# Experts of a decoder layer: a ring of ten weight units, gathers without padding rows, results added into the output, down matrices issued by ScalarE

## The reference

```
h  = x + concat(rmsnorm(pooling mixer), rmsnorm(sparse attention), rmsnorm(memory attention)) @ w_out
hn = rmsnorm(h, g_ffn)
grp = argmax of softmax(hn @ w_router1 + b1)          # one of 4 groups
top 2 of the 8 experts of that group, weights = softmax(top 2) * p(grp)
y  = h + sum over the 2 chosen experts e of  weight * (silu(hn @ w_gate[e]) * (hn @ w_up[e])) @ w_down[e]
```

## Time and profile before

| | us |
|---|---|
| median of 3 runs (1293.37 to 1298.17) | 1296.27 |
| span of the profiled execution, first to last instruction | 1288.5 |
| `mix` begins | 580.8 |
| first gather of `experts` | 720.0 |
| last down product begins | 1253.1 |
| TensorE busy | 1060.3 |
| VectorE busy | 458.5 |
| moved by DMA | 294.33 MB |

### The profile page before, as it was taken

One profiled execution on the slowest core, in us unless ns is written; L12 is line 12 of the kernel. 1 busy time (PEld: TensorE's weight loads), 2 busy tenths in 40 slices (PEclk: granted clock), 3 DMA queues, 4 the chain that ended last, 5 costly groups with the idle time before them and its releaser, 6 DMA issues. The chain is left out here.

```text
span 1288.5 us, 16001 instructions
## 1 busy us (share of the span) xinstructions
PE 1060.3 (82%) x6275; PEld 694.2 (54%) x6275; DVE 458.5 (36%) x950; ACT 175.3 (14%) x415; POOL 71.2 (6%) x104
## 2 busy tenths in 40 slices
PE   5899979999996899988996498788887788877880
PEld 2455657777784677776455354444444444444440
DVE  3233313422424678653434322222222222222223
ACT  1021211111100344330001000000000000000000
POOL 0000030100100000000000100000000000000003
PEclk9999889999976799686996698999999999999995
DMA  9970083553100600004115279999999999999995
GB/s 396 266 231 25 13 199 99 154 141 98 50 1 2 253 1 1 1 1 196 69 63 231 81 284 401 403 400 408 409 404 407 405 407 410 406 413 415 407 382 207
DMA packets 58438, 294.33 MB, mean 228 GB/s; under 512 B 6992, under 2 KB 23183, under 8 KB 40783
## 3 DMA queue, kind: packets, MB, share of 16 engines
q1 hardware_dynamic: 35191, 255.76, 51.8%
q0 software_dynamic: 5280, 21.15, 5.2%
q10 hardware_dynamic: 17920, 16.78, 4.2%
HBM read 272.55 MB, written 25.42 MB: 231 GB/s over the span
## 5 line engine op out<-in xcount | busy, mean ns | idle before, releaser
L1751 PE MATMUL ps<-w_b,xTe 128*64 128x256 f32 x1024 | 132.0, 416 | 37.8 <-DMA w_b<-in_w_up 34.1
L1751 PE MATMUL ps<-w_a,xTe 128*64 128x256 f32 x1024 | 123.2, 397 | 27.0 <-DMA w_a<-in_w_up 24.9
L1813 DVE COPY xTe<-ps 128x512 f32<-128x512 f32 x32 | 22.1, 692 | 345.9 <-PE ps L1741 345.9
L829 PE MATMUL ps<-XT,w_a 128*128 128x126 f32 (+1 forms) x576 | 132.9, 409 | 5.7 <-DVE ht L564 5.7
L829 PEld LDWEIGHTS ps<-XT,w_a 128*128 128x128 f32 x576 | 120.4, 227 | 15.4 <-issue 6.3
L1751 PEld LDWEIGHTS ps<-w_b,xTe 128*64 128x64 f32 x1024 | 81.4, 150 | 83.9 <-DMA w_b<-in_w_up 40.9
L1751 PEld LDWEIGHTS ps<-w_a,xTe 128*64 128x64 f32 x1024 | 74.3, 142 | 71.3 <-DMA w_a<-in_w_up 30.8
L430 PE MATMUL ps<-w_b,xT 128*128 128x454 f32 (+1 forms) x240 | 81.1, 549 | 0.7 <-ACT z L402 0.7
L1856 ACT ACTIVATE gc<-gc 128x256 f32<-128x256 f32 x32 | 13.3, 416 | 450.2 <-DVE gc L1819 450.2
L1726 POOL DMA_INDIRECT xg<-hn_dram,table x32 | 28.8, 899 | 592.6 <-PE ps L1741 453.9
L1378 PE MATMUL ps<-w_b,mT 128*128 128x512 f32 x128 | 58.1, 614 | 1.9 <-ACT mT L1446 1.3
(11 more groups left out here) (362 smaller groups left out, 1308.5 us busy)
## 6 DMA issues: line engine op xcount, KB each, us to landing
w_a<-in_w_gate SPq DMA_DIRECT2D x16, 2048.0 KB, 17.2
w_a<-in_w_up SPq DMA_DIRECT2D x16, 2048.0 KB, 23.3
w_a<-in_w_down SPq DMA_DIRECT2D x16, 2048.0 KB, 12.5
w_b<-in_w_gate SPq DMA_DIRECT2D x16, 2048.0 KB, 16.6
w_b<-in_w_up SPq DMA_DIRECT2D x16, 2048.0 KB, 22.4
w_b<-in_w_down SPq DMA_DIRECT2D x16, 2048.0 KB, 13.2
w_a<-in_cache_kv SPq DMA_DIRECT2D x64, 256.0 KB, 5.1
ys_dram<-yb ACTq DMA_DIRECT2D x64, 128.0 KB, 7.8
```

The source lines that it names most:

```text
L829: ins = nc.tensor.matmul(hidv[:, 2 * q:2 * q + 2, 0:n], w1[:, q, l, :], XT[:, q, :, l:l + 8 * (n - 1) + 1:8], start=(l == 0), stop=(l == 15))
L1751: ins = nc.tensor.matmul(ps[h * CAP:h * CAP + CAP, bank, 0:FH], xT[:, slot, k, :], w[slot][:, k, h * FH:h * FH + FH], start=(k == 0), stop ...
L1813: nc.vector.tensor_copy(xT[:, slot, :, :].rearrange("p k s -> p (k s)"), ps[:, 4, 0:KD * CAP]).then_inc(xT_ready, 1)
```

## The change

What it does, part by part:

- **Ring.** Gate, up and down matrices of all experts become units u = 3n, 3n+1, 3n+2 in one ring of ten buffers: six in `w_a` and `w_b`, two in the space of `z`, two new ones (`more`) that exist only in the `experts` stage. For `z` to be free, GpSimd first copies the part of it that `mix` reads into `zu`, and TensorE and SyncE wait for that. Eight units are loaded in `mix` instead of six.
- **Who issues them.** SyncE issues gate and up units, ScalarE the down units from n = 3 on, behind its exponential of expert n-3.
- **Padding rows.** An unused slot now holds the number 2048 (the first slot of an expert 519), and gathers skip numbers above 519.
- **Adding scatter.** ScalarE multiplies the result by the slot's weight (`slot_w`) as it copies it. GpSimd then adds the 128 half rows of an expert (2 KB each, unused ones skipped) straight into `y` by an indirect transfer with `compute_op=ADD`. Each waits for the one before it to land. `mix` stores `h` to `y` for that.
- **Table.** The product that makes `table` also makes `slot_w`, and both for 128 partitions: 96 columns and 40 passes where there were 48 and 20. The first two gathers are issued at the end of `mix`.
- **Gone.** `combine`, the `h_dram` and `ys_dram` buffers, and the clearing write. `overflow` moves into the `experts` stage. The loops over experts are written out.

The places stand in this order: `mix` (SyncE, GpSimd, TensorE), the two new transfers, then `experts` (SyncE, GpSimd, ScalarE).

```diff
-            wg, wu, wd = self.expert_slot(self.w_a)
-            self.load_gate_up(sp, 0, 0, (wg, wu))
-            self.load_down(sp, 0, 0, wd)
+            for u in range(3):
+                self.load_unit(sp, u)
+            sp.wait_ge(u_kept, 2)
+            for u in range(6, 8):
+                self.load_unit(sp, u)
...
+            nc.gpsimd.tensor_copy(zu[:, 0:TILES, :], z[:, 0:TILES, U0:U0 + 256]).then_inc(u_kept, 1)
+            nc.gpsimd.tensor_copy(zu[0:NB, TILES, :], z[0:NB, TILES, U0:U0 + 256]).then_inc(u_kept, 1)
...
+            pool.wait_ge(table_ready, 1)
...
+            for n in range(2):
+                self.gather(pool, n)
...
-                    ins = nc.tensor.matmul(ps[0:CAP, 0, 0:NTILE], slot_hot[0:r, n, :], tile_tok[0:r, n, :], start=(n == 0), stop=(n == 2 * NT - 1))
+                    for a in range(2):
+                        ins = nc.tensor.matmul(ps[CAP * a:CAP * a + CAP, 0, 0:2 * NTILE], slot_hot[0:r, n, :], tile_hot[0:r, n, :, :].rearrange("p m s -> p (m s)"),
+                                               start=(n == 0), stop=(n == 2 * NT - 1))
...
+    def gather(self, pool, n):
+
+        pool.indirect_dma_start(out=self.xg[0:CAP, n % 2, :], out_offset=None, in_=self.hn_dram,
+                                in_offset=bass.IndirectOffsetOnAxis(ap=self.table[:, n:n + 1].bitcast(U32), axis=0),
+                                bounds_check=NTOK - 1, oob_is_err=False).then_inc(self.xg_in[n % 2], 16)
...
+        def scatter(pool, n, slot, sem):
+
+            pool.indirect_dma_start(out=rows, out_offset=bass.IndirectOffsetOnAxis(ap=self.halves[:, n:n + 1].bitcast(U32), axis=0),
+                                    in_=yb[:, slot, :], in_offset=None, bounds_check=2 * NTOK - 1, oob_is_err=False,
+                                    compute_op=ALU.add).then_inc(sem, 16)
...
-            with sp.Fori(1, NEXP // 2) as i:
-                for slot in range(2):
-                    sp.wait_ge(up_done, i * 4 + 2 * (slot - 1))
-                    self.load_gate_up(sp, i * 2 + slot, slot, (wg[slot], wu[slot]))
-                    sp.wait_ge(y_in_psum, i * 4 + 2 * (slot - 1))
-                    self.load_down(sp, i * 2 + slot, slot, wd[slot])
+            for u in range(8, NU):
+                if u >= RING and u % 3 == 2:
+                    continue
+                if u >= RING:
+                    n, m = (u - RING) // 3, (u - RING) % 3
+                    if m == 0:
+                        sp.wait_ge(gate_done, 2 * n + 2)
+                    elif m == 1:
+                        sp.wait_ge(up_done, 2 * n + 2)
+                    else:
+                        sp.wait_ge(y_in_psum, 2 * n + 2)
+                self.load_unit(sp, u)
...
-                if n >= 2:
-                    pool.wait_ge(x_turned, n - 1)
-                pool.indirect_dma_start(out=xg[:, n % 2, :], out_offset=None, in_=self.hn_dram,
+                if n + 2 < NEXP:
+                    pool.wait_ge(x_turned, n + 1)
+                    self.gather(pool, n + 2)
+                pool.wait_ge(y_copied, n + 1)
+                if n >= 1:
+                    pool.wait_ge(y_out, 16 * n)
+                scatter(pool, n, n % 2, y_out)
...
-                if uses is not None:
-                    act.wait_ge(y_out[slot], uses * 32)
-                nc.scalar.copy(yb[:, slot, :], ps[0:2 * CAP, 6 + slot, :]).then_inc(y_copied, 1)
-                act.wait_ge(y_copied, n + 1)
-                for h in range(2):
-                    act.dma_start(ys[bass.ds(n, 1), :, 512 * h:512 * h + 512].rearrange("o s d -> (o s) d"), yb[h * CAP:h * CAP + CAP, slot, :]).then_inc(y_out[slot], 16)
+                if n >= 2:
+                    act.wait_ge(y_out, 16 * (n - 1))
+                nc.scalar.activation(yb[:, n % 2, :], ps[0:2 * CAP, 6 + n % 2, :], ACT.Copy, scale=self.slot_w[:, n:n + 1]).then_inc(y_copied, 1)
+
+            def load_down(n):
+
+                act.wait_ge(up_done, 2 * (n - 3) + 2)
+                self.load_unit(act, 3 * n + 2)
```

More of the change, by code:

```diff
@@ L131, in constants @@
     c[:, C_TOK:C_TOK + 5] = i[:, None] + P * np.arange(5)[None, :]
+    c[:, C_HALF] = i >= CAP
+    c[:, C_LAST] = np.where(i % CAP == 0, NTOK - 1, FAR)
     for u in range(2):
@@ L1676, in load_down @@
-    def load_down(self, sp, n, slot, w):
-        src = self.ins["w_down"].rearrange("(e h p j) d -> e p h j d", h=2, p=P, j=KF // 2)
-        sp.dma_start(w, src[bass.ds(n, 1), :, :, :, :].rearrange("e p h j d -> (e p) h j d")).then_inc(self.weights_in[2][slot], 16)
+            row = junk[:, 0:NTILE]
+            dve.wait_ge(mixed_ready, NT)
+            ch.then(nc.vector.tensor_scalar(row, ps[:, 0, 0:NTILE], float(FAR), self.c(C_LAST, 1), ALU.add, ALU.min))
+            nc.vector.tensor_copy(self.table[:, :], row[0:CAP, :]).then_inc(table_ready, 1)
@@ new lines, in _, with gate_or_up, down_half, load_unit @@
+            nc.vector.tensor_scalar(self.halves[:, :], row, 2.0, self.c(C_HALF, 1), ALU.mult, ALU.add)
+            nc.vector.tensor_copy(self.slot_w[:, :], ps[:, 0, NTILE:2 * NTILE])
+        self.close(st)
+    def gate_or_up(self, u):
+        return self.units[u % RING].rearrange("p (k f) -> p k f", k=KD)
+    def down_half(self, u):
+        return self.units[u % RING].rearrange("p (h j d) -> p h j d", h=2, d=D)
+    def load_unit(self, sp, u):
+        n, m = u // 3, u % 3
+        if m < 2:
+            src = self.ins[("w_gate", "w_up")[m]].rearrange("(e p k) f -> e p k f", p=P, k=KD)[n]
+            sp.dma_start(self.gate_or_up(u), src).then_inc(self.unit_in[u % RING], 16)
+        else:
+            src = self.ins["w_down"].rearrange("(e h p j) d -> e p h j d", h=2, p=P, j=KF // 2)[n]
+            sp.dma_start(self.down_half(u), src).then_inc(self.unit_in[u % RING], 16)
@@ L1690, in experts @@
         FH = FF // 2
-        wg, wu, wd = zip(self.expert_slot(self.w_a), self.expert_slot(self.w_b))
-        xg = self.sb("xg", [CAP, 2, D], stack=st)
+        more = self.sb("more", [P, RING - 8, UNIT], stack=st)
+        self.units += [more[:, j, :] for j in range(RING - 8)]
         xT = self.sb("xTe", [P, 2, KD, CAP], stack=st)
-        gc = self.sb("gc", [2 * CAP, 2, FF // 2], stack=st)
-        hh = self.sb("hh", [2 * CAP, 2, FF // 2], stack=st)
+        gc = self.sb("gc", [2 * CAP, 2, FH], stack=st)
@@ L1773, in down, with turn_h @@
                             ins.then_inc(y_in_psum, 1)
-            def turn_h(n, slot):
+            def turn_h(n):
                 pe.wait_ge(hh_ready, n + 1)
-                turn(5, hh[:, slot, :], KF // 2).then_inc(h_turned, 1)
-            turn_x(0, 0, 1, first=True)
-            gate_up(0, 0, 1)
-            turn_x(1, 1, 1)
-            turn_h(0, 0)
-            gate_up(1, 1, 1)
-            turn_x(2, 0, 2)
-            down(0, 0, 1, first=True)
-            turn_h(1, 1)
-            with pe.Fori(1, NEXP // 2 - 1) as i:
-                for slot in range(2):
-                    n = i * 2 + slot
-                    gate_up(n, slot, i + 1)
-                    turn_x(n + 1, 1 - slot, i + 1 + slot)
-                    down(n + (-1), 1 - slot, i + slot)
-                    turn_h(n, slot)
@@ L1794, in _ @@
-            n, half = NEXP - 2, NEXP // 2
-            gate_up(n, 0, half)
-            turn_x(n + 1, 1, half)
-            down(n - 1, 1, half - 1)
-            turn_h(n, 0)
-            gate_up(n + 1, 1, half)
-            down(n, 0, half)
-            turn_h(n + 1, 1)
-            down(n + 1, 1, half)
+                turn(5, hh[:, n % 2, :], KF // 2).then_inc(h_turned, 1)
+            turn_x(0)
+            for n in range(NEXP):
+                gate_up(n)
+                if n + 1 < NEXP:
+                    turn_x(n + 1)
+                if n >= 1:
+                    down(n - 1)
+                turn_h(n)
@@ new lines, in _ @@
+            down(NEXP - 1)
+            with needed(pe):
+                pe.wait_ge(y_copied, NEXP)
+                with pe.Fori(0, NOVER) as j:
+                    pe.wait_ge(o_xg_in, j * 16 + 16)
+                    turn(4, xg[0:CAP, 0, :], KD).then_inc(o_x_turned, 1)
+                    pe.wait_ge(o_xT, j + 1)
+                    pe.wait_ge(o_w_in, j * 48 + 48)
+                    for u in range(2):
+                        for k in range(KD):
+                            for h in range(2):
+                                ins = nc.tensor.matmul(ps[h * CAP:h * CAP + CAP, 2 * u, 0:FH], xT[:, 0, k, :], self.gate_or_up(u)[:, k, h * FH:h * FH + FH],
+                                                       start=(k == 0), stop=(k == KD - 1))
+                    ins.then_inc(o_gate_up, 1)
+                    pe.wait_ge(o_hh, j + 1)
+                    turn(5, hh[:, 0, :], KF // 2).then_inc(o_h_turned, 1)
+                    pe.wait_ge(o_hT, j + 1)
+                    for k in range(KF):
+                        h, i = k // (KF // 2), k % (KF // 2)
+                        for a in range(2):
```

(13 more changed lines are left out.)

406 lines of the change are left out of this document (143 added, 263 removed).

## The result

The changed kernel takes 1460.26 us (median of 6 runs, 1445.48 to 1461.32) against 1297.22 for the kernel before: a ratio of 1.121, 95% interval 1.115 to 1.127. It is slower by 12%, where 1320 (+1.8%) was predicted and 1243 to 1385 was the range. The profiled execution, the fastest of the six, took 1445.5 us, with a span of 1443.6, and its sums are made in that span.

The account below looks back on a forecast made before the run. The prediction saw the old experts paced by transfers and the changed ones by a closed chain through scatter and gather: 765.7 + 31 periods of 17.6 us is 1311, plus 7.8 makes 1319, said as 1320; range 1243 to 1385.

Parts of the forecast that it names:

- the mechanism: Between down products: a closed chain of copy, scatter issue, gather landing, transposes and down product decides, 7.3 us + L.
- Rival 1: In the experts: the gather comes in time and transfers set the pace, 1235 to 1276 us; chance 0.36.
- L: Time from a gather's start to its landing: taken as 10.3 us, with ends of 8.4 and 16.
- Rival 2: In the experts: scatter rows take a third queue's turns, L 12 to 15, P 19.3 to 22.3, 1372 to 1465 us; chance 0.15.
- P: Period from one expert's down product to the next: 17.6 us forecast, ends 15.7 and 23, 16.86 for no change.
- the scatter's share of L: Scatter rows ahead of the gather in its queue: 1 to 2.5 us, less 1.2 head start; 4 at worst.
- the +1.4: Added to the earlier 8.9 us landing for scatter rows ahead, a third queue and skipped rows, giving L = 10.3.
- the down product: TensorE's last step in each period's chain, priced at 3.65 us.
- The third queue: Down matrices issued from another queue at the same moment as the gather: 0 to 3 us more landing.
- The first transposes: Ahead of the experts: their start moves from 723.84 to about 727.6 us, +3.7.
- the end: After the last down product: copy, last scatter and barrier take 9 us in place of 31.7.
- Transfers of a period: DMA work per expert: weights 14.5, gather 1.1, adding write 0.55, in sum 16.1 us; bounds 15.4 and 17.3.

Follow-up runs that it names:

- Run 1: Changed kernel with GpSimd issuing the gather of expert n+4 ahead of its wait for the result of expert n: 1267.76 us, 0.979 of the kernel before.
- run 3: Changed kernel with unused slots gathering row 519 instead of being skipped, 64 rows per gather: 1474.53 us, 1.139 of the kernel before.
- run 4: Changed kernel with every scatter row out of bounds and skipped, the instructions kept: 1441.03 us, 1.113 of the kernel before.
- run 6: Changed kernel with gather n+3 issued ahead of the scatter of n, both still behind ScalarE's copy: 1296.23 us, 0.9995 of the kernel before.
- Run 2: Changed kernel with the down matrices issued by SyncE again, in order of use: 1457.88 us, 1.126 of the kernel before.
- run 8: Changed kernel with a scatter that overwrites instead of adding: 1385.95 us, 1.070 of the kernel before.
- run 5: Kernel before, with each gather from expert 3 on also waiting for ScalarE's copy of the result of n-3: 1285.45 us, ratio 0.993.
- run 10: Changed kernel with gathers issued two experts earlier and all down matrices issued by SyncE: 1260.39 us, 0.971 of the kernel before.
- 11: Changed kernel with gathers two experts earlier, down matrices by SyncE and an overwriting scatter: 1231.3 us, 0.949 of the kernel before.
- run 7: Changed kernel with SyncE issuing gate and up matrices of n+4 only once the gather of n+3 has landed: 1360.7 us, 1.051 of the kernel before.

## Why the prediction was wrong

**What was right.** The direction (0.53 for slower) and the mechanism: GpSimd holds the gather behind the scatter, the scatter behind ScalarE's copy, and TensorE waits at the transposes of x and not for weights. Run 1 shows that with the gather let go earlier the whole loss is gone. Rival 1 would have needed L below 9.3. The numbers are those of Rival 2, at 0.15: its L of 12 to 15 (12.3), its P of 19.3 to 22.3 (21.7 in the mean of all 31), TensorE's wait of over 5 us and the half clock behind it. Its reason, the turns of a third queue, is not what came: the turns are with SyncE's packets.

**The steps that failed** are two terms of the sum that were sized too small, by 2 us each. The first is the scatter's share of L, "a like number of rows ahead costs 1 to 2.5 us, less the 1.2 us head start", and the +1.4 taken from it. It was priced from two stores of ScalarE's queue, which are other packets in another queue. The right unit was the packet on one DMA engine: nine of them at 0.585 us each, less 1.9, or +3.4; L came out at 12.3 for 10.3. Skipped rows save 1.0 of landing (run 3), as the low end had it, but a skipped scatter row saves next to nothing (run 4). The second is the down product, taken at 3.65 although the forecast itself has TensorE wait 3 to 4 us ahead of it; it takes 5.7. This isn't only the first miss over again: in run 6, with L at 9.0 and a wait of 3.1 us, it still takes 5.1. By estimate, 31 periods with either miss alone give some 1380 us, inside the range; both together, with the smaller terms below, leave it.

**The third queue** was given 0 to 3 us "at the same moment". It isn't the same moment. ScalarE's issue stands behind an exponential that comes after the gather's landing, which the order of VectorE's list would have told. Run 2 puts it at nothing.

**The terms around L.** In the steady periods (17.6 predicted, 22.98 measured):

| term | predicted | measured |
|---|---|---|
| ScalarE's copy, with the 0.07 ahead | 0.65 | 0.76 |
| GpSimd's start after it | 0.3 | 0.82 |
| from the scatter's start to the gather's | 1.25 | 1.86 |
| landing L, with the step to TensorE | 10.4 | 12.3 |
| transposes | 1.38 | 1.42 |
| down product | 3.65 | 5.7 |
| sum | 17.6 | 22.9 |

The copy, the start, the issue and the transposes are those of the period shown above, L is the median and the product the mean of the stretch. The scatter was priced as a gather of 128 rows. Nearly all of the miss on it is the adding: run 8's overwriting scatter takes 1.01 us, which with the gap of 0.30 makes 1.31, and the adding one 1.55, or 1.86. The start after a copy was read from a gap between two gathers that wait for nothing; behind another engine it is 0.8. The down product follows a wait of 8 us, and its granted clock is 0.57 in the period shown; over 800 to 1200 us it is 0.80 where it was 0.97. The half clock stood in rival 2 alone, at 1.7; the forecast, with its own wait of 3 to 4 us, should have had it too: the row with a wait of 2.50 us already shows it. Not every wait brings it: in run 5 TensorE waits 1.86 us for an up matrix at 1108.49, and the 32 passes behind take 3.67 us, the full clock's time. L (+1.9), the product (+2.0), the issue (+0.6), the start (+0.5) and the copy (+0.1) make 5.1 of the 5.4 us per period.

**Outside the periods** little was off. The first transposes came at 725.13 where 727.6 was expected, and the end took 12.7 us, not 9: copy, start and scatter are done after 5.2, sooner than the 5.6 put for them, but the overflow test and the barrier take 7.5, not 3. For the last two periods 3 us were taken off; the last three saved 39.6 against full ones (3 x 22.98 less 29.4), because without a gather the chain is not there.

**Transfers of a period** were put at 16.1 us (15.4 to 17.3). In run 10, where they set the pace, the period is 16.04 (24 of them from 809.36 to 1194.36), so that sum was good, and with it what the change could have brought. Its upper end was not: with no rows saved and the write doubled, the prediction's own terms give 14.5 + 1.1 + 2.2 = 17.8. The rule on adding transfers, cited from Collectives: The Full Stack, section "The bandwidth ceiling: the fold count and why AG ≠ RS ≠ AR", in the Trainium skill, stands there for the ReduceScatter of a ring. Applied to half the rows it doubles a write of 0.55, which is the 16.1 and not the upper end that the prediction named for it. Here adding costs 0.44 us of a period by the traces of runs 10 and 11.

**What stays open.** Why the old kernel gains 0.7% by a later gather. What adding costs, better than 14 to 29 us. And L without any weights under way at the same point, which run 7 missed.

## What to carry to other kernels

Before an instruction is put behind another in a queue, draw the closed chain from one result to the next, and price the landing in it by packets per DMA engine in the same queue, each with one packet of every other busy queue, not by bytes: a skipped row counts too. A prefetch must never stand behind the store of a result that isn't made yet when nothing but the order of the list asks for it. Where a chain makes TensorE wait for several microseconds, price the passes behind the wait by rows at the lower clock level as well.

## What the hardware showed unexpectedly

- A scatter whose 128 rows are all out of bounds makes the same number of packets (7632 in GpSimd's queue) as one that moves its rows, and lands hardly sooner: 10.7 us where 11.5 is usual.
- An adding indirect transfer of 128 rows of 2 KB is 9 packets on each DMA engine, an overwriting one 5, for the same bytes; GpSimd spends 1.55 us on the first and 1.01 on the second.
- Two instructions of one queue, swapped, moved the time by 11% (1460.3 to 1296.2), though together they move under 5% of the bytes.
